# Layer norm sums and first chunks, gate chunks and scaled probabilities in a two-block transformer kernel

## The reference, cut to what matters

```python
o_a = _dsa_branch(...)            # softmax attention, 8 heads of 64, causal, top 128 keys
o_b = _stick_breaking_branch(...) # 8 heads of 64
y_a = jnp.matmul(o_a.reshape(b, s, WIDTH_A), w_branch_a[i])
y_b = jnp.matmul(o_b.reshape(b, s, WIDTH_B), w_branch_b[i])
merged = jax.nn.sigmoid(gate_a) * y_a + jax.nn.sigmoid(gate_b) * y_b
x = x + jnp.matmul(merged, w_out[i])
```

```python
for l in range(DEPTH_2):
    mix = _even_mixer(...) if l % 2 == 0 else _odd_mixer(...)
    h = _layernorm(DN_ALPHA * h + mix, ln_mix_g[l], ln_mix_b[l])
    f = jnp.square(jax.nn.relu(h @ mlp_w1[l])) @ mlp_w2[l]
    h = _layernorm(DN_ALPHA * h + f, ln_mlp_g[l], ln_mlp_b[l])
```

## Time and profile before

| | us |
|---|---|
| median of 3 runs | 2762.01 (2761.5 to 2762.05) |
| the profiled execution, its own time | 2744.34 |
| its span, first to last instruction | 2742.6 |

### The profile page before, as it was taken

The page is one execution under the profiler, slowest core; times in us unless marked ns, Lnnn a source line. Parts: engine busy times, 40 slices in busy tenths (PEclk is TensorE's granted clock), DMA queues, the critical chain, the costliest instruction groups (busy, mean ns, idle before and its releaser), DMA issues.

```text
span 2742.6 us, 30358 instructions
## 1 busy us (share of the span) xinstructions
PE 2586.7 (94%) x11768; PEld 1758.7 (64%) x11768; DVE 788.4 (29%) x1294; ACT 693.1 (25%) x1116; POOL 597.0 (22%) x362
## 2 busy tenths in 40 slices
PE   7999999899799979998989999989999999899998
PEld 3446554445433334785679999978877567677875
DVE  0551332111311122234136216135100231640622
ACT  1302224410111121145232222132322231421222
POOL 0000001110011100011004344324433013344442
PEclk9799998899799989999999999999999999999999
DMA  3121110034589952220012222222222012222220
GB/s 139 47 77 65 42 49 10 0 118 174 221 324 356 387 238 70 73 77 8 31 39 93 85 91 86 84 70 93 93 84 77 24 43 81 71 91 92 92 92 31
DMA packets 68261, 275.33 MB, mean 100 GB/s; under 512 B 12440, under 2 KB 12568, under 8 KB 55872
## 3 DMA queue, kind: packets, MB, share of 16 engines
q1 hardware_dynamic: 59648, 260.01, 25.7%
q0 software_dynamic: 8512, 13.89, 1.5%
HBM read 321.02 MB, written 16.80 MB: 123 GB/s over the span
## 4 chain that ended last, share of the span: by engine, by line
PE 45%; issue 22%; POOL 6%; DVE 1%; ACT 1%; DMA 1%; POOLq 0%; SPq 0%; DVEq 0%
PE ps L739 14%; PE ps L754 13%; PE ps L1121 6%; POOL weights_low L2243 5%; PE ps L723 3%; PE ps L1143 3%; PE ps L637 2%; PE ps L469 1%; PE ps L1107 1%; PE ps L661 1%; PE ps L629 1%; DMA area<-pair_rows 0%; POOL parts L2243 0%; PE ps L1129 0%; PE ps L780 0%
## 5 line engine op out<-in xcount | busy, mean ns | idle before, releaser
L754 PE MATMUL ps<-parts 128*128 128x512 f32 x1920 | 486.1, 398 | 26.1 <-DVE parts L1639 13.6
L2243 POOL TENSOR_TENSOR parts<-weights,parts 128x1024 fp32r<-128x1024 f32 x128 | 325.5, 2543 | 632.2 <-ACT parts L1557 632.2
L739 PE MATMUL ps<-parts 128*128 128x264 f32 x3328 | 425.9, 286 | 16.2 <-DVE parts L1787 6.8
L754 PEld LDWEIGHTS ps<-parts 128*128 128x128 f32 x1920 | 364.7, 190 | 118.2 <-issue 24.5
L739 PEld LDWEIGHTS ps<-parts 128*128 128x128 f32 x3328 | 417.7, 191 | 17.7 <-issue 15.6
L1557 ACT ACTIVATE parts<-weights 128x1024 fp32r<-128x1024 f32 x192 | 202.8, 1056 | 427.3 <-PE ps L739 155.5
L2243 POOL TENSOR_TENSOR weights_low<-weights,parts 128x1024 fp32r<-128x1024 f32 x64 | 156.5, 2445 | 317.8 <-ACT parts L1557 317.8
L1121 PE MATMUL ps<-area,normed 128*64 128x512 f32 x752 | 172.8, 601 | 1.6 <-DVE normed L1975 1.6
L1787 DVE TENSOR_TENSOR parts<-normed,parts 128x528 f32 (+1 forms) x64 | 159.0, 2484 | 9.4 <-DVE normed L1786 2.1
L458 PE MATMUL ps<-normed,weights 128*128 128x512 f32 x288 | 125.7, 599 | 3.1 <-DVE normed L1609 2.4
L1121 PEld LDWEIGHTS ps<-area,normed 128*64 128x64 f32 x752 | 56.3, 139 | 112.5 <-issue 110.3
(11 more groups left out here) (371 smaller groups left out, 3180.7 us busy)
## 6 DMA issues: line engine op xcount, KB each, us to landing
weights<-in_weights SPq DMA_DIRECT2D x283, 512.0 KB, 3.5
area<-in_experts SPq DMA_DIRECT2D x141, 1024.0 KB
area<-pair_rows SPq DMA_DIRECT2D x4, 1024.0 KB, 8.0
residual<-in_x SPq DMA_DIRECT2D x1, 2048.0 KB, 9.7
area<-bias_scratch POOLq DMA_DIRECT2D x1, 2048.0 KB, 8.6
token_rows<-area SPq DMA_DIRECT2D x1, 2048.0 KB, 6.6
out_tiles<-residual SPq DMA_DIRECT2D x4, 512.0 KB, 2.8
area<-in_decay POOLq DMA_DIRECT2D x2, 528.0 KB, 3.8
```

The costliest lines, as they stand in the source:

```text
L739: ins = mm(ps[:, b + h, 0:HALF], wt[:, k], x[:, m * DT + k, HALF * h:HALF * h + HALF], start=m == k == j == 0, stop=m == chunks - 1 and k ...
L754: ins = mm(ps[:, b], wt[:, k], x[:, m * DT + k, META:T2], start=m == k == j == 0, stop=m == chunks - 1 and k == DT - 1 and j == 2)
L2243: g.tensor_tensor(low, RING[:, n % SLOTS], place[0][n % 2], ALU.subtract).then_inc(S["w_lo"], 1)
```

## The change

**Layer norm and RMS sums.** `NONES` (a matrix of -1) is turned into 1/1024 once the stick-breaking branch is done, and named `MEAN`. A new `total` on VectorE adds tiles 0 to 6 into `R` while the stage before the norm runs; TensorE adds `R` and tile 7 only. VectorE subtracts the mean straight from PSUM. The two RMS sums at L570 and L642 do the same with the squares (`rms_sum`).

**Parts.** High parts get four slots in the MLPs, low parts always lie in `RING_LOW`. The first four chunks of the stage behind the norm are rounded before the norm. In the norm ScalarE writes the eight high tiles first and `x` after, VectorE does all eight multiplications and then the low tiles, from `HN` and the bias. TensorE's new `first_pair` takes two chunks at once: first all matmuls with the high tiles, for each as it comes, then those with the low tiles. In the MLP's first matmuls ScalarE evacuates a tile before it rounds the next chunk, not after. VectorE's accumulations in the MLP are written out instead of looped.

**Gates.** Two gate chunks for each pair of heads stay in the first branch, a quarter chunk per unit; the other eight go to the stick-breaking branch, two for each pair, in shares of 3, 3, 2 and 0 of the 8 matmuls a unit, into PSUM bank 7.

**Probabilities.** VectorE scales the exponentials in place by the inverse sum, and the transposes become real ones (`is_transpose`) against the identity.

```diff
+        MEAN = NONES
...
-        FH, FL = part(0, 16, N2), part(8448, 16, N2)
-        XH, XL = part(16896, DT, N2), part(21120, DT, N2)
-
-        IN_MLP = [[part(25344 + D * j, D) for j in range(2)], [part(25344 + D * (2 + j), D) for j in range(2)]]
+        XH, XL = part(0, DT, N2), part(4224, DT, N2)
+        FH, FL = part(12544, 16, N2), part(20992, 16, N2)
+
+        IN_MLP = [[part(8448 + D * j, D) for j in range(4)], None]
...
+        EARLY = {use_of("odqk") + 2 + j: part(D * j, D) for j in range(2)}
...
+            def first_pair(high, low, place, cols):
+
+                banks = [2 * bank() for _ in range(2)]
+                pair = [take_parts(place) for _ in range(2)]
+                for k in range(DT):
+                    pe.wait_ge(S["x_hi"], w.next("x_hi"))
+                    for c in range(2):
+                        for h, at, width in cols:
+                            for j in range(2):
+                                ins = mm(ps[:, banks[c] + h, 0:width], pair[c][j][:, k], high[:, k, at:at + width],
+                                         start=k == j == 0, stop=False)
+                                if k == c == h == j == 0:
+                                    begun(ins)
+                for c, k in [(c, k) for k in range(DT - 2) for c in range(2)] + [(c, k) for c in range(2) for k in (DT - 2, DT - 1)]:
+                    if c == 0:
+                        pe.wait_ge(S["x_lo"], w.next("x_lo"))
+                    for h, at, width in cols:
+                        ins = mm(ps[:, banks[c] + h, 0:width], pair[c][0][:, k], low[:, k, at:at + width],
+                                 start=False, stop=k == DT - 1)
+                        if c == 1 and h == 0 and k == DT - 2:
+                            begun(ins)
+                    if k == DT - 1:
+                        ins.then_inc(S["tile_done"], 1)
+
...
+            def layer_norm(cols):
+
+                pe.wait_ge(S["sum_part"], w.next("sum_part"))
+                for j, src in enumerate((R, X[:, DT - 1])):
+                    if j:
                         pe.wait_ge(S["dve_evac"], w.value("dve_evac"))
-                    ins = mm(ps[:, 0], ONES, XA[:, t], start=t == 0, stop=t == DT - 1)
+                    for h, at, width in cols:
+                        x = R[:, at - cols[0][1]:at - cols[0][1] + width] if j == 0 else src[:, at:at + width]
+                        ins = mm(ps[:, h, 0:width], MEAN, x, start=j == 0, stop=j == 1)
...
+            def rms_sum(last):
+
+                pe.wait_ge(S["sum_part"], w.next("sum_part"))
+                mm(ps[:, 7], ONES, R[:, 0:SEQ], start=True, stop=False)
+                pe.wait_ge(S["norm_sq"], w.next("norm_sq", 8))
+                mm(ps[:, 7], ONES, last, start=False, stop=True).then_inc(S["norm_sum"], 1)
...
+                        for k in range(2 * (u % 4), 2 * (u % 4) + 2):
+                            ins = mm(ps[:, 5 + u // 4], gate.wt[:, k], HA[:, k], start=k == 0, stop=k == DT - 1)
...
-                            ins = mm(ps[:, 2 + u % 2, P * k:P * k + P], EX[u % 2][:, P * k:P * k + P], DG[u % 2],
-                                     start=True, stop=True)
+                            ins = mm(ps[:, 2 + u % 2, P * k:P * k + P], EX[u % 2][:, P * k:P * k + P], IDENT,
+                                     is_transpose=True, start=True, stop=True)
...
+                    def gate(u):
+
+                        first, last = ((0, 3), (3, 6), (6, 8), (8, 8))[u % 4]
+                        if first == 0:
+                            pe.wait_ge(S["dve_evac"], w.value("dve_evac"))
+                            w.count("dve_evac")
+                            gate.wt = take()
+                        for k in range(first, last):
+                            ins = mm(ps[:, 7], gate.wt[:, k], HA[:, k], start=k == 0, stop=k == DT - 1)
+                            if k == 0:
+                                begun(ins)
+                            if k == DT - 1:
+                                ins.then_inc(S["tile_done"], 1)
...
+                            gate(u)
+                            after(u)
...
+                act.wait_ge(S["lru_done"], 4)
+                for j in range(4):
+                    high(use_of("up0") + j, slots=-1)
...
+                parts = XH if kind == "mix" else XHO if l == 0 else None
+                if parts is not None:
+                    for t in range(DT):
+                        act.wait_ge(S["norm_out"], w.next("norm_out"))
+                        fn(parts[:, t, T2 - T:], h[:, t], ACT.Identity, bias=vec(f"ln_{kind}_b", 8 * l + t)).then_inc(S["x_hi"], 1)
                 for t in range(DT):
-                    act.wait_ge(S["norm_out"], w.next("norm_out"))
...
+            def high(n, i=None, place=IN_MLP, slots=None):
+
+                turn, back = n // SLOTS + 1, (slots or len(place[0])) - 2
                 act.wait_ge(chunk_full[n % SLOTS], (turn if i is None else i + turn) * 16)
-                act.wait_ge(S["chunk_begun"], n if i is None else i * SLOTS + n)
-                fn(place[0][n % 2], RING[:, n % SLOTS], ACT.Copy).then_inc(S["w_hi"], 1)
+                if slots is None or slots > 0:
+                    act.wait_ge(S["chunk_begun"], n - back if i is None else i * SLOTS + n - back)
+                fn(high_slot(n, place), RING[:, n % SLOTS], ACT.Copy).then_inc(S["w_hi"], 1)
...
+            def total(n, x, T, name, waits):
+
+                if 1 <= n < DT - 1:
+                    dve.wait_ge(S[name], waits)
+                    ins = v.tensor_tensor(R[:, 0:T], x[:, 0] if n == 1 else R[:, 0:T], x[:, n], ALU.add)
+                    if n == DT - 2:
+                        ins.then_inc(S["sum_part"], 1)
+                    else:
+                        step(ins)
+
...
-                if l:
-                    step(v.tensor_scalar(R[:, 0:T], ps[:, 0], 1.0 / D, None, ALU.mult))
-                else:
-                    step(v.tensor_scalar(two(R[:, :]), halves(0), 1.0 / D, None, ALU.mult))
                 for t in range(DT):
-                    v.tensor_tensor(h[:, t], x[:, t], R[:, 0:T], ALU.subtract).then_inc(S["ln_cent"], 1)
+                    if l:
+                        ins = v.tensor_tensor(h[:, t], x[:, t], ps[:, 0], ALU.subtract)
+                    else:
+                        ins = v.tensor_tensor(two(h[:, t]), two(x[:, t]), halves(0), ALU.subtract)
...
+                        if between is gate_out:
+                            probs = EX[u % 2][:, 0:P * (order[u] + 1)]
+                            v.tensor_scalar(probs, probs, st[:, 3:4], None, ALU.mult).then_inc(S["diag"], 1)
...
```

211 lines of the change are left out of this document (107 added, 104 removed).

## The result

The changed kernel takes 2673.74 us (median of 4 runs, 2670.21 to 2685.74) against 2762.03 us before in the same series (4 runs, 2761.5 to 2767.18). The ratio is 0.9684, 95% interval 0.9649 to 0.9719. The forecast was 2697 us, range 2668 to 2727, faster: the direction and the range held, and the time came out 23 us lower than forecast. From profiled execution to profiled execution it is 2744.34 to 2677.25, 67 us, where the sum said 65; from lowest time to lowest time of all series it is 2744.02 to 2670.21, 73.8 us.

What follows compares the result with a forecast made beforehand. TensorE, busy for 94% of the span, was taken as the bound, so only removed matmuls, waits or low clock could give time. 23 + 10 + 17 + 55 - 40 = 65 us off the 2762 us median gave 2697 us, range 2668 to 2727.

Steps and rivals of the forecast that it cites:

- the sum: Whole kernel: gains of 23, 10, 17 and 55 us less a cost of 40, together 65 us less.
- taken from the median, 2762 - 65: Whole kernel: the 65 us subtracted from the median of 2762.0, 17.7 us above the profiled execution, giving 2697 us.
- Branches: Attention branches: 55 us less in the first, 40 us more in the stick-breaking one, from moving half the gate chunks.
- the chain through VectorE: First branch: TensorE waits for scaled probabilities behind bias, maximum, reciprocal and scaling, 1.7 us a pass.
- low-clock episode: First branch: a stretch at the lower TensorE clock costing 1.6 us, counted in all four passes.
- its low-clock term: Stick-breaking branch: full clock returns after some 4.5 us rather than 13.7, 2.3 us lost a pass.
- Sums of the norms: Four layer norms: running totals on VectorE and a ready-scaled mean save 5.8 us each, 23 us.
- The two RMS norms: Sums before two RMS norms: the same running totals save 5.4 and 4.5 us, 10 us together.
- First two chunks: Behind three layer norms: 7.8 us less each, minus 2 us for low clock, 17 us in all.
- A: Rival, chance 0.20: stick-breaking branch stays at 1.2 GHz for 13.7 us of each pass, 18 us worse, 2715 us.
- B: Rival, chance 0.16: clock hardly falls; stick-breaking branch 9, first branch 6, norms 6 us better, 2676 us.
- C: Rival, chance 0.04: gaps drop the first branch to 1.2 GHz, 25 us worse in each of four passes, 2798 us.

Runs made afterwards that it cites:

- before_again: The kernel before, with no edit, run again for a second trace: median 2756.77 us, 0.9994 of the time before.
- after_again: The changed kernel run once more with no edit, giving its second trace: median 2671.04 us, 0.9697 of the time before.
- late_gates: Changed kernel with the stick-breaking branch's gate products moved late in each group of four units: median 2686.59 us, 0.9765 of the time before.
- gap_filled: Changed kernel with each stick-breaking pass's first gate share ahead of the wait for staged operands: median 2662.24 us, 0.9667 of the time before.
- sums_undone: Changed kernel with TensorE again summing all eight tiles in the six norms, no running totals: median 2717.36 us, 0.9884 of the time before.
- both_filled: Changed kernel with the first gate share ahead of the staged-operand wait in both branches: median 2655.06 us, 0.9611 of the time before.
- late_rounding: Changed kernel with the fourth early-rounded weight chunk put back behind the inverse deviation: median 2678.64 us, 0.9702 of the time before.

## Why the prediction was right, and where it was off

- **Direction and size.** The sum was 65 us; the profiled executions differ by 67.1, the lowest times by 73.8. The forecast time was 23 us too high. Of that, 14.5 us are the step "taken from the median, 2762 - 65": it took the offset of 17.7 us between profile and median for something that the changed kernel keeps, and that kernel's median is only 3.5 us over its lowest time. The offset was low-clock stretches of the kernel before (before_again). The other 8.8 us are in the terms of the sum, most of it in the first two chunks. That the profiled executions differ by nearly the sum is partly luck: that of the changed kernel took 6.5 us more than its second traced run, at a clock of 0.964 beside 0.968.
- **Branches**: 55 less and 40 more forecast, 55.4 and 38.5 found (after_again). The first branch is right for reasons that offset in part: the chain through VectorE was put at 6.8 us and is 2.8 to 3.0, and the transposes fell from 23.0 to 15.3 (7.7, where I took 2.1 a pass, 8.4). The low-clock episode that I counted in all four passes stands in two of them in the first trace (passes of 32.4, 33.7, 32.3 and 33.6 us) and in three in the second. In the other branch 39.4 us a pass was forecast and 37.8 to 40.0 found (36.6 to 39.9 in the second trace); late_gates and gap_filled show that its low-clock term was argued from the right thing.
- **Sums of the norms**: the layer norms were put at 23 us and gave 5.9 + 5.9 + 5.7 + 5.7 = 23.2. The two RMS norms gave 8.7 (10 forecast). The second gave 3.6 of 4.5, since its two groups run at the low clock, and 1.7 us more go behind it. The sum had no term for that idle time and its clock. *sums_undone* lost 30.9 of the 33 that I expected, since its edit leaves the 0.7 us a norm on VectorE saved.
- **First two chunks**: 17 us forecast, 8.2 + 6.8 + 8.1 = 23.2 found. The 7.8 us by rows was right; the 2 us a site that I took off for a low clock had the wrong sign, since less idle time stood ahead of the chunks. The rest of the gain, some 1.6 us, is stretches at another clock elsewhere.
- **Rivals.** A (gates don't hide) needed a clock near 0.8; it is 0.93. B is what happened at the norms (6 us better than the sum, 6.2 found), but the branches were as forecast, not as in B. That its time (2676) is nearest is luck: the offset of the median made the difference. C, in which the first branch falls to 1.2 GHz through its short gaps, didn't come: gaps of 0.35 us stand twice in each pass and its clock is 0.97. The Trainium skill ("TensorE: Matmul & The Clock Gate", "A second HAM failure mode: psum-queue depth-cycling") has an engine that idles briefly swing between its clocks. Inside the two branches the traces agree with it only at the 1.6 to 1.8 us of the pass boundaries, not at each of them, and there filling the idle time kept the full level (gap_filled, both_filled).

## What to carry to other kernels

Price an idle stretch of TensorE with the low clock that follows it, and put dense matmuls that wait for nothing into or right behind it: the same 1.6 to 1.8 us gap was followed by 3 to 7 us at the low level (once by none) with a dense share behind it, by 10 to 14 with small products first, and by none when filled. Move sums of a norm off the path by running totals, and let the first products behind it need as little as possible (here the high part alone, for two chunks). Look for VectorE operations that would start while GpSimd has a long one. Compare a stage between its own first and last instruction in both traces before its column is read as its cost. Before a sum is laid against a median, look at the granted clock of the runs: a profiled execution can lack episodes that most runs have.

## What was not expected of the hardware

- The kernel before has executions from 2744.0 to 2772.9 us, at granted clocks from 0.960 down to 0.947, with the same waits where they were compared (branch 2). Between its two traces the longer low-clock stretches stand in branch 2, in the first mixer and behind norms. One of over 40 us was seen in a single trace (both_filled, 11 us longer to sq1 than gap_filled), in small matmuls with short waits. What sets them off wasn't found.
- A VectorE operation that reads both operands from SBUF and starts while GpSimd computes a low part of the weights (2.3 to 3.0 us) lasts until behind its end. In after_again each of the 70 VectorE additions, subtractions and multiplications of over 2 us ends 0.54 to 0.57 us behind a low part's end. A multiplication of a 128x528 tile takes 0.69 us from start to start; three took 4.22 us in the earlier trace rows, and one of these alone 2.86. In after_again the 64 subtractions of L1858 have a median of 2.66 us and a least of 0.69, and the last running total behind the second mixer took 2.87 us, where such an addition takes 0.69. *late_rounding* moves a low part back in between the multiplications, and at each of its sites one multiplication takes 2.89 us again. The accumulations that read one operand from PSUM (`residual<-residual,ps`) take 0.69 to 0.71 us in after_again, beside GpSimd or not.
